# A hybrid layer on one core: Strassen's product over all eight inner tiles of the input projection, keys and values in rings, merged sums in memory

## What is computed

```python
proj = x @ w_in                    # 2048 x 1024 by 1024 x 9216
(q_sb, k_sb, v_sb, g_sb, u_pool, g_pool, u_lru, g_lru, q_xa, g_xa, merge) = _split_columns(proj)
y_sb = stick_breaking_attention(q, k, v) * silu(g_sb)          # 4 heads of 128, blocks of 128 keys
y_pool = multiscale_pool(u_pool, w_pool, pool_scale) * silu(g_pool)
y_lru = rg_lru(u_lru, ...) * silu(g_lru)                       # convolution, gates, scan over time
y_xa = memory_cross_attention(q_xa, mem, w_mem_kv) * silu(g_xa)
merged = sum(sigmoid(merge)[:, :, n] * (branches[n] @ w_branch[n]) for n in range(4))
return layer_norm(DN_ALPHA * x + merged @ w_out, ln_g, ln_b)
```

## Time and profile before

| what | value |
|---|---|
| runs, median (2 runs) | 2543.82 us (2539.79 to 2547.85) |
| profiled execution, its own time | 2544.53 us |
| its span (first to last instruction) | 2542.4 us |
| granted TensorE clock, mean | 0.993 of full speed |
| busy: PE / DVE / ACT / POOL | 98% / 51% / 45% / 48% |

### The profile page before, as it was taken

How to read it: one execution, slowest core, us unless ns; L and a number is a source line. 1 busy time by engine, 2 the same in 40 slices (tenths; PEclk the granted TensorE clock), 3 DMA queues, 4 the chain that set the end, 5 groups by cost and what they waited for, 6 DMA issues and landing times.

```text
span 2542.4 us, 30074 instructions
## 1 busy us (share of the span) xinstructions
PE 2485.0 (98%) x10928; PEld 2003.2 (79%) x10928; DVE 1287.5 (51%) x1871; ACT 1148.1 (45%) x1830; POOL 1212.8 (48%) x943
## 2 busy tenths in 40 slices
PE   8999999999999999999999999999999999999998
PEld 6888788888877888887777777688878877888886
DVE  5555642531683265264677677722531683265264
ACT  5555632342573245232567677732342573245231
POOL 3555543654335534544555455543654345534533
PEclk9999999999999999999999999999999999999999
DMA  6222211111111111142302111011111111112133
GB/s 245 83 84 83 67 50 46 59 51 42 48 52 50 48 50 60 51 174 91 133 34 83 59 59 67 17 50 46 58 50 42 49 52 50 48 50 61 34 108 108
DMA packets 53859, 171.08 MB, mean 67 GB/s; under 512 B 6096, under 2 KB 10192, under 8 KB 52688
## 3 DMA queue, kind: packets, MB, share of 16 engines
q1 hardware_dynamic: 45360, 147.66, 17.7%
q10 hardware_dynamic: 8352, 21.50, 2.4%
HBM read 146.59 MB, written 22.54 MB: 67 GB/s over the span
## 4 chain that ended last, share of the span: by engine, by line
PE 84%; DVE 6%; issue 4%; POOL 3%; DMA 2%; ACT 2%; SPq 0%; POOLq 0%; ACTq 0%; DVEq 0%
PE J L498 18%; PE J L500 17%; PE J L499 17%; PE Z L684 6%; PE OB L654 5%; PE ACC L684 3%; PE OB L684 3%; PE Z L498 2%; PE Z L499 1%; PE Z L500 1%; PE ACC L631 1%; PE ACC L633 1%; PE ACC L643 1%; PE ACC L641 1%; DVE XBL L1350 1%
## 5 line engine op out<-in xcount | busy, mean ns | idle before, releaser
L498 PE MATMUL J<-XBH,WH 128*128 128x512 f32 x1584 | 627.8, 396 | 8.1 <-DVE XBL L1350 3.2
L499 PE MATMUL J<-XBL,WH 128*128 128x512 f32 x1584 | 618.8, 391 | 0.0
L500 PE MATMUL J<-XBH,WL 128*128 128x512 f32 x1584 | 618.7, 391 | 0.0
L498 PEld LDWEIGHTS J<-XBH,WH 128*128 128x128 f32 x1584 | 298.9, 189 | 78.9 <-issue 7.4
L499 PEld LDWEIGHTS J<-XBL,WH 128*128 128x128 f32 x1584 | 298.6, 189 | 63.9 <-issue 3.8
L500 PEld LDWEIGHTS J<-XBH,WL 128*128 128x128 f32 x1584 | 298.3, 188 | 63.3
L1856 POOL TENSOR_TENSOR WL<-RAW,WH 128x512 fp32r<-128x512 f32 x142 | 204.6, 1441 | 283.3 <-ACT WH L835 282.6
L1938 POOL TENSOR_TENSOR PLO<-PF,PHI 128x512 fp32r<-128x512 f32 (+3 forms) x160 | 179.9, 1124 | 152.2 <-DVE PHI L1520 146.2
L498 PE MATMUL J<-XBH,WHS 128*128 128x512 f32 x576 | 229.1, 398 | 20.0 <-DVE LG L1359 9.0
L500 PE MATMUL J<-XBH,WLS 128*128 128x512 f32 x576 | 227.3, 395 | 0.0
L499 PE MATMUL J<-XBL,WHS 128*128 128x512 f32 x576 | 227.2, 395 | 0.0
(11 more groups left out here) (373 smaller groups left out, 5085.4 us busy)
## 6 DMA issues: line engine op xcount, KB each, us to landing
RAW<-w SPq DMA_DIRECT2D x144, 512.0 KB, 3.6
BRAW<-w SPq DMA_DIRECT2D x64, 256.0 KB, 3.9
XRAW<-xt SPq DMA_DIRECT2D x16, 512.0 KB, 11.6
OR<-w SPq DMA_DIRECT2D x16, 512.0 KB, 4.5
RES<-xrow SPq DMA_DIRECT2D x16, 512.0 KB, 4.4
out<-RES SPq DMA_DIRECT2D x16, 512.0 KB, 2.7
MW<-w SPq DMA_DIRECT2D x8, 512.0 KB, 8.4
pk_q<-ST SPq DMA_DIRECT2D x8, 512.0 KB, 2.7
```

The lines of the kernel that those rows point to most:

```text
L498: nc.tensor.matmul(to, wh, xh, start=first, stop=True, skip_group_check=True)
L499: nc.tensor.matmul(to, wh, xl, start=False, stop=True, skip_group_check=True)
L500: return nc.tensor.matmul(to, wl, xh, start=False, stop=True, skip_group_check=True)
```

## The change

- `piece`: all eight inner tiles go by Strassen's form: 7 products of 4 inner tiles, so 14 pieces of 6 matmuls. The blocks of x become 14 units (6 plain, 8 sums) where there were 11 (7 plain, 4 sums); each takes a high part and a rest, and the sums are now made by DVE alone.
- Banks: a and c share two banks in turn, d has the third. Piece 10 waits for the copy of product 4, made by piece 7. ACT copies behind its pieces 1, 3, 7, 11; DVE adds behind 5, 9, 11, 13.
- Weights: the raw sums are 4 operations of 128x512 on POOL and two halves of WHS/WLS of 128x1024. WL1 (whole, at DVE's piece 6) and WL2 (at its piece 1) go from POOL to DVE. In `quiet` pairs (lru and M2) DVE makes both halves of WLS and WL2, POOL makes WL1.
- Keys are split once, written to memory as high part and rest, and read back by SP block by block in a ring of 5; values in a ring of 7. They were read whole by ACT and split by ACT and DVE.
- The merged sums are kept in memory: SP writes each GT tile out and reads the former sum to MB; DVE adds. GT is free for ACT only when the write has landed (`wait_kept`).
- Hooks move with the pieces: `memory_turned` ahead of piece 8 (was 9), `memory_values` 11 (12), `rest_y` of M2+1 behind 9 (8), `convolve` behind 9 (8). At the start the four value tiles of the memory are split later, and their products run inside the first pair, ahead of piece 4.

```diff
-PIECES = 15
...
-BLOCK_OF = (B11, T1, B21, P10, P00, T2, B22, P11, P01, T3, T4, P10, P00, P11, P01)
...
+PIECES = 14
+PRODUCTS = 7
...
+NU = 14
...
+NK, NV = 5, 7
...
-                a, c, d = (J[(g + j) % 3] for j in range(3))
+                a, c, d = J[g % 2], J[(g + 1) % 2], J[2]
...
+                elif i == 6:
                     pe.wait_ge(cp_done, 4 * g + 1)
...
+                elif i == 8:
+                    pe.wait_ge(s_lo, 2 * g + 2)
                     pe.wait_ge(cp_done, 4 * g + 2)
...
+                elif i == 10:
                     pe.wait_ge(cp_done, 4 * g + 3)
...
+                elif i == 12:
+                    pe.wait_ge(t_lo, g + 1)
                     pe.wait_ge(ad_done, 4 * g + 1)
...
+                to, w, w0 = ((a, ONE, 0), (c, SUMMED, 0), (d, ONE, 4), (a, SUMMED, 4), (c, SUMMED, 8), (a, SUMMED, 12),
+                             (d, TWO, 0))[i // 2]
+                mm = block_product(to, w, w0 + i % 2 * 2, i, i in (0, 2, 4, 12))
+                if i % 2:
+                    mm.then_inc(pr_done, 1)
...
                 for h in range(HEADS):
-                    pair(g0 + XA0 + h, {9: lambda: memory_turned(half, h - 1),
-                                        12: lambda: memory_values(half, h - 1)} if h else {})
+                    pair(g0 + XA0 + h, {8: lambda: memory_turned(half, h - 1),
+                                        11: lambda: memory_values(half, h - 1)} if h else {})
...
+                elif i == 1:
                     room(g, 0)
                     shared(g, 0, 0, 0, 1)
-                elif i == 1:
+                elif i == 2 and g % PAIRS < 2 * HEADS and g % 2:
+                    split_keys(g)
+                elif i == 3:
                     room(g, 1)
...
-                    first_tile(g + 1, False)
-                elif i == 5:
+                elif i == 5 and not last:
+                    first_tile(g + 1)
+                elif i == 7:
                     shared(g, 0, 1, 0, 4)
-                elif i == 8 and not last:
-                    first_tile(g + 1, True)
-                elif i == 9:
+                elif i == 9 and not last:
+                    sums_of(g + 1, False)
+                elif i == 11:
                     shared(g, 1, 0, 0, 6)
-                    if not last:
...
+            def rest_of_first(g):
+                if g > GLAST:
+                    return
+                dve.wait_ge(w_hi, 4 * g + 1)
+                wait_if(dve, a_lo, g)
+                V_.tensor_tensor(WL1[:], RAW[0][:], WH1[:].bitcast(F32), ALU.subtract).then_inc(a_lo, 1)
...
-                if i == 0 and low_on_dve(g):
+                l = g % PAIRS
+                if i == 1:
                     rest_of_second(g)
-                if i == 9 and low_on_dve(g + 1):
-                    rest_of_sums(g + 1)
-                if i in (4, 8, 12, 14):
-                    summed(g, (4, 8, 12, 14).index(i))
-                if g % PAIRS < 2 * HEADS and g % 2 and i in (11, 14):
+                    if quiet(g) or l == 0:
+                        rest_of_sums(g, True)
+                if i == 3 and l < 2 * HEADS and l % 2:
+                    rest_keys(g)
+                if i in (5, 9, 11, 13):
+                    summed(g, (5, 9, 11, 13).index(i))
+                if i == 6 and l + 1 < PAIRS and not quiet(g + 1):
+                    rest_of_first(g + 1)
+                if i == 10 and quiet(g + 1):
+                    rest_of_sums(g + 1, False)
...
+            def load_k(half, gs):
+                h, s = (gs - first_step(half, 0)) // NS[half], (gs - first_step(half, 0)) % NS[half]
+                if s == 0:
+                    sp.wait_ge(k_kept, 32 * (half * HEADS + h + 1))
+                wait_if(sp, z_done, gs - NK + 1)
+                sp.dma_start(KR[gs % NK][:].bitcast(F32), pk_k[h, :, STEPS[half][s][1]]).then_inc(k_in[gs % NK], 16)
...
+            def load_merged(half, n, f):
+                wait_kept(sp, half, n - 1, f)
+                wait_if(sp, merged, add_count(half, n, max(f - 1, 0)))
+                sp.dma_start(MB[f % 2][:], pk_m[f]).then_inc(mb_in[f % 2], 16)
+            def keep_merged(half, n, f):
+                if n:
+                    sp.wait_ge(merged, add_count(half, n, f + 1))
+                else:
+                    sp.wait_ge(mu_done, f_count(half, n, f + 1))
+                sp.dma_start(pk_m[f], GT[f % 4][:]).then_inc(m_kept[f % 4], 16)
+            def exchange(half, n, f):
+                for j in (f, f + 1):
+                    if n < NB - 1 or j < KEPT:
+                        keep_merged(half, n, j)
+                    if n and j + 2 < FT:
+                        load_merged(half, n, j + 2)
...
+            def add(half, n, f):
+                if n == 0:
+                    return
+                dve.wait_ge(mu_done, f_count(half, n, f) + 1)
+                dve.wait_ge(mb_in[f % 2], 16 * (half * 12 + (n - 1) * 4 + f // 2 + 1))
+                wait_if(dve, merged, add_count(half, n, f))
+                to = MERGED[:, f, :] if n == NB - 1 and f >= KEPT else GT[f % 4][:]
+                V_.tensor_tensor(to, MB[f % 2][:], GT[f % 4][:], ALU.add).then_inc(merged, 1)
...
-                pair(g0 + 1, {8 if n == 2 else 4: lambda: rest_y(half, n)})
+                pair(g0 + 1, {9 if n == 2 else 4: lambda: rest_y(half, n)})
                 for i in range(2, 4):
-                    gated(half, n, 2 * i - 4)
-                    gated(half, n, 2 * i - 3)
+                    for f in (2 * i - 4, 2 * i - 3):
+                        gated(half, n, f)
+                        add(half, n, f)
...
+            def sum_raw(g, j):
+                a11, a12, a21, a22 = RAW[0][:, 0:4], RAW[0][:, 4:8], RAW[1][:, 0:4], RAW[1][:, 4:8]
+                a, b, op = ((a21, a22, ALU.add), (SR[:, 0:4], a11, ALU.subtract), (a12, SR[:, 4:8], ALU.subtract),
+                            (a11, a21, ALU.subtract))[j]
+                pool.wait_ge(w_raw[0] if j else w_raw[1], 16 * (g + 1))
+                pool.wait_ge(pr_done, PRODUCTS * (g - 1) + (2, 4, 5, 6)[j])
+                pool.wait_ge(s_raw, 4 * g + j)
+                G_.tensor_tensor(SR[:, 4 * j:4 * j + 4], a, b, op).then_inc(s_raw, 1)
```

1140 lines of the change are left out of this document (590 added, 550 removed).

## The result

The changed kernel takes 2658.74 us (2656.23 to 2661.26, 2 runs) against 2543.82 before: a ratio of 1.0452, 95% interval 1.0369 to 1.0535. It is slower by 115 us where I forecast it 41 us faster. The profiled execution took 2661.26 us, with a span of 2659.5.

What follows compares the result with a forecast made beforehand. PE, busy 2485.0 of 2542.4 us, was taken to bound the kernel. From 2544.5, saved matmuls (-97.9) and new costs (+22 + 7 + 12 + 10 + 3 + 6 - 3) gave 2503 us, 8 in 10 from 2468 to 2540.

Steps and rivals of the forecast that it cites:

- Fewer matmuls: 72 pairs have 14 pieces of 6 matmuls instead of 15: 97.9 us less if nothing waits anew.
- Merged sums in memory: Merges: GT is free once SP's write lands; most waits hidden, 12 pairs at 0.5 us: +6 (0 to 17).
- xa pairs: PE's transposes wait about 2 us for DVE's normalisation behind WL1; with clock, eight pairs at 2.75: +22 (12 to 35).
- M2+1: In each half PE waits up to 3.2 us for DVE's YL and 1.7 for ACT's copy, plus clock: +12 (3 to 16).
- lru pairs: DVE's chain with larger WLS and WL2 loses most of the 1.36 us saved a pair: 8 x 0.9, +7 (2 to 14).
- First pairs: More units, rests and sums on DVE at the start, +10 (5 to 13), and at the change of halves, +3 (-4 to +8).
- Keys and values in rings: The V wait of 2.1 us goes, and ACT's splits of keys with it: -3 (-5 to 0).
- The covers hold: Rival: chains have slack the rows don't show, so new waits add only 16 us: 2462; chance 0.17.
- The bank chain: Rival: in attention, piece 10 waits for ACT's late copy of product 4; 36 us more, about 2540; chance 0.16.
- SP's queue: Rival: a wait on the keys' write at a ring's head delays loads behind it; 56 us more, 2559; chance 0.06.
- The prediction's own sign of being wrong: Wrong if PE's new waits and half clock sum to under 25 us or over 90.

Runs made afterwards that it cites:

- e1: Changed kernel with SP writing and reading the merged sums ahead of the pair, and so of the weights' load, instead of behind piece 4: 2590.84 us.
- e6: On e5, the last merge's second exchange of merged sums also put ahead of the loads on SP: 2542.34 us.
- e3: Changed kernel with DVE's subtraction WL1 put behind the normalisation in the pairs in which PE turns the memory weights: 2628.35 us.
- e9: On e8, the second merge's four rests YL put on DVE behind piece 7 instead of 9: 2530.01 us.
- e8: On e7, DVE's variance put behind its sum of piece 11 in the lru pairs, instead of ahead of it: 2542.53 us.
- e11: On a later version with variance back in its old place, POOL's WL1 put behind the second raw sum in the lru stage: 2532.78 us.
- e13: As e11, and DVE's scan (recur) also put behind piece 1 of the next pair: 2522.84 us.
- e5: Changed kernel with the edits of e1 and e3, and in the lru stage the weights' sums earlier on ACT, DVE and POOL: 2555.91 us.
- e15: On a version with several lists reordered, the last but one rows' normalisation put behind piece 9 of the second half's first pair: 2533.43 us.
- e16: Fastest version (2519.55 us) with two of the convolution's three multiply-add steps left out, as a test of DVE's work: 2505.14 us.
- e17: Fastest version (2519.55 us) with POOL's WL1 in the lru stage made for one inner tile of eight: 2513.0 us.
- e7: On e6, POOL made to wait in each half's first pair for DVE's rests XBL before the next pair's raw sums: 2535.88 us.

## Why the prediction was wrong, step by step

**Fewer matmuls, -97.9.** Right in count, and nearly in price: the pool stage, with only 1.2 us of waits, fell by 9.0 us where 8 pairs at 1.36 make 10.9.

**Merged sums in memory, +6 (0 to 17): the step that failed.** The writes' place in SP's list alone measured 82 us (e1 and e6). The step had the order of the queue wrong: it put the next weights' loads behind the write, but the first of them stands ahead of it, and its condition is DVE's WL2. So the write was issued 8.7 us behind the end of its addition, where the step has the issue 3.4 to 5.0 behind the gate's end. It had WL2 directly behind the addition, at 0.7 us; it stands behind the second addition, and took 2.87. The addition took 1.80 for 1.2, and the landing 5.1 for 2.7. The count of 12 pairs was right: 12 of PE's 18 waits stand in them, at 4.0 to 4.4 us each where 0.5 was taken. Four of 0.6 to 0.9 are in the first merge, which writes its sums too and which the step left out, and two of 5.4 are in M2+1. The order could be read from the code, the price of a subtraction beside another from the earlier trace rows. With this term right, the sum would have been 2503 + 76 = 2579, slower by over 1%, and outside my range.

**xa pairs, +22 (12 to 35).** Right in mechanism, somewhat small: e3 gained 30 us by moving the one instruction that the step named, and PE's wait was 3.0 a pair where 2.0 was taken. In the first such pair PE asks 11.1 us behind the pair's start (10.9 forecast); WL1 began 1.0 us later than forecast, and the first group of multiplications took 1.95 for 1.14. One reading of the earlier trace rows was wrong, though the sum doesn't rest on it: the transposes and the normalisation did not meet "within 0.03 us". PE's first eight transposes need only the first group, which had ended at 959.62, 3.3 us earlier; the second eight began at 963.79, 0.9 behind the second group. And the row of 3.14 us, held there against a rule on two inputs, is of an instruction with one tensor input.

**M2+1, +12 (3 to 16).** The YL part is borne out: PE waited 3.9 us in each half where up to 3.2 was taken, and e9 gained 12.5 by moving it. The part on ACT was not tested by itself; PE's wait for ACT's copy in M2+1 was 5.4 in each half, but 3.8 in e1 with the writes mended, and the kernel before had one of 4.3 to 4.4 there too (GT). So an additional 1.7 isn't seen.

**lru pairs, +7 (2 to 14).** Too small: 18.3 us over nominal in the stage, and more in M2 behind it, where the last recurrence ends. The step took about 1 us more a pair for the larger WLS and WL2; at 723.97 a single WLS took 2.28 where it takes 1.22 alone. The timelines suggest a loop: DVE's WL2 lets the load go, POOL sums and subtracts, ACT makes the high part, then the decays, DVE's variance and the sum. That it is one chain isn't shown, since moving its members (e8, e11 to e13) brought none of the gains that this theory gave. With the writes mended, the orders of the lists that I tried (e5 to e15) have the lru stage and the merge behind it at 468 to 485 us together, both halves, against 468.9 before and a nominal 447.3. That less work on DVE or on POOL shortens it is shown by e16 and e17; which order would be best is open.

**First pairs, +13.** 23.0 over nominal, 18.0 of it in the first half, whose first pair ended at 72.0 where 64.7 was forecast. Part of the reason is seen in e7: the rests were priced at 1.21 us, and four of them cost 2.5 each beside POOL's sums. Without that the first pair was 5.2 us shorter, but the second 5.7 longer.

**Keys and values in rings, -3.** Wrong in the sum, though the V wait went. The stages of the heads and the first merge are 23.4 us over nominal. e1 gives back 4.6 of that; 18.8 stay. In the second half the six pairs of the heads behind the first two took 311.5 us before and 311.5 after, so nothing of their saving of 8.2 arrived; PE's waits from 1300 to 1750 rose from 3.5 to 10.7 us. They are many and short (in the whole kernel ARG 4.9 us in 14 places, PLO 3.0 in 4), and no run tested them: open.

**The rivals.** "The covers hold" failed everywhere but in the pool stage. "The bank chain" named the line that leads PE's waits, copies by ACT, but put it in the attention, behind activations; the waits stand in the merges, behind a DMA. "SP's queue" had the mechanism, a conditional entry that holds what is behind it, and 0.06: I had looked for it at the loads of K and V, for which PE never waits, and not at the new writes behind the old load.

**The whole.** 57 us of new losses were forecast, 214.8 came. 76 of the missing 158 are the writes. Of the other 82, some 22 are in the heads and the first merge, without a tested cause, 12 in xa, 11 in lru and 10 in the first pairs. Several rows were priced at the duration of an engine that runs alone (the additions, WL2, the rests of the first pair); how much of the 82 is theirs wasn't measured. The prediction's own sign of being wrong, new waits and half clock over 90 us, came with 142 and 62. Nearly a third of it all is clock, which the terms did contain (0.4 us for each of waiting; measured 62 for 142).

## What to carry to other kernels

When a write is added to an in-order queue, read off what stands ahead of it there and on what that waits; if the write's own condition is met earlier, it belongs ahead. Here that order alone was worth 82 us, nearly as much as the 97.9 us of matmuls that the change saved. When work goes from POOL to DVE or back, price it at the duration beside the other engine (2.3 to 2.9 us for a DVE rest that takes 1.2 or 0.7 alone), and expect it to lengthen what the other does. A saving on the bounding engine is only worth what the covers have left: this kernel's gave way in every stage but one, and the best order found keeps 24 of 98 us.
